# Spatial mixing woven into the projections of a one-core transformer kernel

## What is computed

```
h = rmsnorm(x, mix_norm)
q, k, v, su, sv, g_a, g_b = split(h @ w_in)
# chunked spatial gating: 4 chunks of 128 tokens, 8 groups of 64 channels
v = rmsnorm(gelu(sv), sgu_norm)
w = where(causal, w_s, 0)                                   # 8 x 128 x 128
mixed = einsum('gij,bcjgd->bcigd', w, v_chunks) + b_s
y_sgu = gelu(su) * mixed
y_att = sliding_window_attention(q, k, v, ...)              # 8 heads of 64, window 128
merged = sigmoid(g_a) * (y_att @ w_oa) + sigmoid(g_b) * (y_sgu @ w_ob)
x = x + merged @ w_out
```

## Time and profile before

| | |
|---|---|
| median of three runs | 1462.38 us |
| the profiled execution | 1462.21 us |
| its span, first to last instruction | 1460.5 us |
| busy: TensorE, VectorE, ScalarE, GpSimd | 1353.8, 779.4, 515.0, 605.4 us |
| mean granted TensorE clock | 0.978 |

### The profile page before, as it was taken

The page is one execution under the profiler, slowest core; times in us unless marked ns, Lnnn a source line. Parts: engine busy times, 40 slices in busy tenths (PEclk is TensorE's granted clock), DMA queues, the critical chain, the costliest instruction groups (busy, mean ns, idle before and its releaser), DMA issues.

```text
span 1460.5 us, 20168 instructions
## 1 busy us (share of the span) xinstructions
PE 1353.8 (93%) x6757; PEld 1085.5 (74%) x6757; DVE 779.4 (53%) x1526; ACT 515.0 (35%) x1084; POOL 605.4 (41%) x367
## 2 busy tenths in 40 slices
PE   4998799999899999999988699999979999999987
PEld 2765577687688888888867487777857888888866
DVE  3323667554455655641232467777524766666661
ACT  2222233411333333320111466666401544444420
POOL 3431133236344444465533244444244555555521
PEclk9999999999999999999999899999999999999999
DMA  5241122223133332333332011111123322222102
GB/s 150 79 95 44 44 72 58 72 59 101 58 101 98 89 100 87 100 105 94 94 98 72 14 45 44 29 43 43 29 77 92 97 69 70 68 68 68 57 20 82
DMA packets 196544, 105.38 MB, mean 72 GB/s; under 512 B 18974, under 2 KB 194428, under 8 KB 196492
## 3 DMA queue, kind: packets, MB, share of 16 engines
q1 hardware_dynamic: 195968, 103.98, 25.0%
q0 software_dynamic: 432, 0.69, 0.2%
q10 hardware_dynamic: 92, 0.02, 0.0%
HBM read 102.57 MB, written 2.10 MB: 72 GB/s over the span
## 4 chain that ended last, share of the span: by engine, by line
PE 78%; DVE 8%; issue 5%; ACT 4%; POOL 3%; DMA 1%; SPq 0%; DVEq 0%; POOLq 0%; ACTq 0%
PE ps L349 18%; PE ps L350 18%; PE ps L351 18%; PE ps L371 9%; PE ps L1164 1%; PE ps L1175 1%; POOL w_low L336 1%; PE ps L858 1%; DMA w_raw<-in_w_in_dram 1%; PE ps L1192 1%; PE ps L1194 1%; PE ps L1193 1%; POOL y_low L635 1%; PE ps L842 1%; DVE scaled L469 1%
## 5 line engine op out<-in xcount | busy, mean ns | idle before, releaser
L336 POOL TENSOR_TENSOR w_low<-w_raw,w_high 128x1024 fp32r<-128x1024 f32 x183 | 447.5, 2446 | 598.5 <-DVE w_high L331 598.4
L349 PE MATMUL ps<-h_high,w_high 128*128 128x512 f32 x864 | 353.4, 409 | 16.4 <-DVE h_low L473 11.6
L350 PE MATMUL ps<-h_low,w_high 128*128 128x512 f32 x864 | 344.0, 398 | 0.0
L351 PE MATMUL ps<-h_high,w_low 128*128 128x512 f32 x864 | 342.6, 397 | 0.0
L331 DVE CAST w_high<-w_raw 128x1024 fp32r<-128x1024 f32 x183 | 136.5, 747 | 154.8 <-PE ps L351 70.7
L349 PEld LDWEIGHTS ps<-h_high,w_high 128*128 128x128 f32 x864 | 164.1, 190 | 64.1 <-issue 20.3
L351 PEld LDWEIGHTS ps<-h_high,w_low 128*128 128x128 f32 x864 | 164.1, 190 | 37.6
L350 PEld LDWEIGHTS ps<-h_low,w_high 128*128 128x128 f32 x864 | 164.1, 190 | 35.3 <-issue 1.0
L1968 DVE SCALAR_TENSOR_TENSOR z<-ps,cv,z 128x511 f32<-128x511 f32 x44 | 33.0, 750 | 97.8 <-ACT z L1463 97.8
L1463 ACT ACTIVATE z<-ps,cv 128x512 f32<-128x512 f32 x44 | 34.3, 779 | 121.9 <-PE ps L351 121.7
L351 PE MATMUL ps<-m_high,w_low 128*128 128x512 f32 x176 | 69.4, 395 | 0.0
(11 more groups left out here) (326 smaller groups left out, 2541.8 us busy)
## 6 DMA issues: line engine op xcount, KB each, us to landing
w_raw<-in_w_in_dram SPq DMA_DIRECT2D x150, 256.0 KB, 3.2
w_raw<-in_w_up_dram SPq DMA_DIRECT2D x88, 256.0 KB, 3.2
w_raw<-in_w_out_dram SPq DMA_DIRECT2D x44, 256.0 KB, 3.0
w_raw<-in_w_down_dram SPq DMA_DIRECT2D x32, 256.0 KB, 3.1
w_raw<-in_w_down_dram SPq DMA_DIRECT2D x16, 192.0 KB, 2.6
rel<-in_rel_bias_dram SPq DMA_DIRECT2D x8, 384.0 KB, 3.1
x_tok<-in_x_dram SPq DMA_DIRECT2D x4, 512.0 KB, 5.6
w_raw<-in_w_oa_dram SPq DMA_DIRECT2D x8, 256.0 KB, 4.2
```

Source lines behind the costliest of these rows:

```text
L336: pool.tensor_tensor(w_low[:, n % RING, :], w_raw[:, n % RAW, :], w_high[:, n % RING, :].bitcast(F32), ALU.subtract).then_inc(low_made, 1)
L349: pe.matmul(acc, wh, mh, start=first and k == 0, stop=False)
L350: pe.matmul(acc, wh, ml, start=False, stop=False)
L351: done = pe.matmul(acc, wl, mh, start=False, stop=last and k == tiles - 1)
```

## The change

- The transposes of `ws_raw` go behind strip 5, into the middle of the su and sv strips; ACT copies them to `ws_t` between the squares of sv and the root of their sum.
- The sums no longer stand behind a projection but inside the next one: projection 1 is cut in four parts with one sv sum behind each; projections 2 to 5 are cut in two with the sum of the projection before between them. `qkv_sum` of the last one stands between the first two quarters of the mixing.
- sv is transposed in projections 4 and 5 (two chunks ahead of each, banks 2 and 3), and VectorE copies the chunks between its normalisations.
- Mixing (`mix`) does for each q and each chunk two matmuls of 64 output partitions and 128 columns, one for each group, so that a q fills one bank (2, 3, 7, 4) and four can be in flight. VectorE (`mixed`) adds the bias, multiplies, rounds and subtracts, each over all 128 partitions; ACT's rounding is gone. All `mix` calls are issued ahead of the first gate strip, with the first scores between the second and the third. VectorE prepares the attention bias ahead of `mixed(0)` and masks the first scores between `mixed(1)` and `mixed(2)`. TensorE's waits for the banks are spread over the first tiles.
- The merge uses w_ob before w_oa: its first strip waits only for the last masked scores, and the second for the whole attention output. The strips' order in memory loads and the banks follow.
- The small attention tensors no longer lie over `ws_raw` and `ws_t`.

```diff
@@ strip_sources
-                if m % 2 == 0:
+                if m % 2 == 1:
@@ tensor: su/sv strips
                 product(pe, ps[:, n % 4, :], n, 0, P, KT, hx).then_inc(strip_used, 1)
+                if n == 5:
+                    pe.wait_ge(s["ws_cut"], 1)
+                    pe.wait_ge(s["gain_ready"], 2)
+                    for g in range(8):
+                        mm = pe.transpose(ps[:, 6 + g // 4, (g % 4) * P:(g % 4 + 1) * P], ws_raw[:, g, :], ident[:])
+                    mm.then_inc(s["ws_turned"], 1)
@@ tensor: projections
+            def sv_turn(c):
+                if c == 0:
+                    pe.wait_ge(s["sv_normed"], 4)
+                elif c == 1:
+                    pe.wait_ge(s["v_ready"], 1)
+                else:
+                    pe.wait_ge(s["sv_tok_ready"], c - 1)
+                for k in range(4):
+                    mm = pe.transpose(ps[:, 2 + c % 2, k * P:(k + 1) * P], uv[:, 4 + k, c * P:(c + 1) * P], ident[:])
+                mm.then_inc(s["sv_turned"], 1)
+
+            cuts = [[(0, 8)], [(0, 3), (3, 5), (5, 7), (7, 8)], [(0, 5), (5, 8)], [(0, 4), (4, 8)], [(0, 4), (4, 8)],
+                    [(0, 4), (4, 8)]]
             for m in range(6):
                 n = N_QKV + m
                 pe.wait_ge(low_made, n + 1)
                 if m >= 4:
                     pe.wait_ge(s["i1_normed"], 1) if m == 4 else pe.wait_ge(s["v_copied"], 1)
-                product(pe, ps[:, bank[m], :], n, 0, P, KT, hx).then_inc(strip_used, 1)
-                if m == 0:
+                if m == 1:
                     pe.wait_ge(s["gelu_done"], 8)
-                    for k in range(4):
-                        sv_sum(k)
-                    qkv_sum(0)
                 elif m == 2:
...
+                    pe.wait_ge(s["ws_ready"], 1)
+                elif m == 4:
+                    sv_turn(0)
+                    sv_turn(1)
+                elif m == 5:
+                    sv_turn(2)
+                    sv_turn(3)
+                for part, ks in enumerate(cuts[m]):
+                    mm = product(pe, ps[:, bank[m], :], n, 0, P, KT, hx, ks=ks)
+                    if ks[1] == KT:
+                        mm.then_inc(strip_used, 1)
+                    if m == 1:
+                        sv_sum(part)
+                    elif m >= 2 and part == 0:
+                        qkv_sum(m - 2)
...
@@ tensor: mixing
+            MIX_BANK = (2, 3, 7, 4)
+
+            def mix(q):
+                if q < 2:
+                    pe.wait_ge(s["sv_tok_ready"], 4)
+                else:
+                    pe.wait_ge(s["i1_normed"], q + 1)
                 for c in range(4):
-                    mm = pe.matmul(ps[:, 2 + 2 * (q % 2) + c // 2, (c % 2) * 256:(c % 2) * 256 + 256],
-                                   uv_tok[:, c, q * P:(q + 1) * P],
-                                   ws_t[:, 2 * q:2 * q + 2, :].rearrange("p g i -> p (g i)"), start=True, stop=True)
+                    for h in range(2):
+                        mm = pe.matmul(ps[h * 64:(h + 1) * 64, MIX_BANK[q], c * P:(c + 1) * P],
+                                       uv_tok[:, c, q * P + h * 64:q * P + (h + 1) * 64], ws_t[:, 2 * q + h, :],
+                                       start=True, stop=True)
                 mm.then_inc(s["mixed"], 1)
...
+            mix(0)
+            qkv_sum(4)
+            mix(1)
+            pe.wait_ge(s["i1_root"], 5)
             a_scores(0, 0, first=True)
+            mix(2)
+            mix(3)
             with pe.Fori(0, 3) as j:
                 a_pair(j)
@@ tensor: merge
-            after(pe, "att")
+            pe.wait_ge(s["a_masked"], 32)
...
-                for b in range(2):
-                    n = N_MERGE + 2 * u + b
+                for turn, b in enumerate((1, 0)):
+                    n = N_MERGE + 2 * u + turn
                     pe.wait_ge(low_made, n + 1)
+                    if u == 0 and turn == 1:
+                        after(pe, "att")
@@ vector: mixing
+            def mixed(q):
                 dve.wait_ge(s["mixed"], q + 1)
...
+                part = scaled[:, q % 2, 0:S].rearrange("p (c i) -> p c i", c=4)
+                dve.tensor_tensor(part, ps[:, (2, 3, 7, 4)[q], :].rearrange("p (c i) -> p c i", c=4),
+                                  bias_s[:, q:q + 1, :].broadcast_to([P, 4, P]), ALU.add).then_inc(s["mix_biased"], 1)
+                dve.wait_ge(s["mix_biased"], q + 1)
+                dve.tensor_tensor(uv[:, q, :], uv[:, q, :], scaled[:, q % 2, 0:S], ALU.mult).then_inc(s["mix_gated"], 1)
+                dve.wait_ge(s["mix_gated"], q + 1)
+                dve.tensor_copy(a_high[:, 4 + q, :], uv[:, q, :]).then_inc(s["mix_high"], 1)
                 dve.wait_ge(s["mix_high"], q + 1)
                 dve.tensor_tensor(a_low[:, 4 + q, :], uv[:, q, :], a_high[:, 4 + q, :].bitcast(F32),
                                   ALU.subtract)
...
             a_bias(0)
+            mixed(0)
+            i1_norm(4)
+            mixed(1)
             a_masked(0, 0, N_GATE + 3)
+            mixed(2)
+            mixed(3)
```

More of the change, by code:

```diff
@@ L809, in _ @@
[L809 to L824, removed]
+                    pe.wait_ge(s["ws_ready"], 1)
[13 more added lines that the diff above has]
+                        qkv_sum(m - 2)
+                    if m == 2 and part == 0:
+                        pe.wait_ge(s["v_copied"], 1)
+                        for t in range(4):
+                            mm = pe.transpose(ps[:, 3, t * P:(t + 1) * P], v_f[:, t * P:(t + 1) * P], ident[:])
+                        mm.then_inc(s["v_turned"], 1)
@@ L865, in a_pair @@
                     pe.wait_ge(low_made, j * 4 + (N_GATE + t + 1))
+                    if t == 3:
+                        pe.wait_ge(s["i1_normed"], 5)
+                    elif t:
+                        pe.wait_ge(s["mix_biased"], t + 2)
                     product(pe, ps[:, GATE_BANK[t], :], N_GATE + t, 0, P, KT, hx, ks=(0, 7))
@@ L1360, in _ @@
                 act.activation(sq[:, k % 2, 0:S], uv[:, 4 + k, :], ACT.Square).then_inc(s["sv_sq"], 1)
+            act.wait_ge(s["ws_turned"], 1)
+            act.activation(ws_t[:].rearrange("p (b g) i -> p b (g i)", b=2), ps[:, 6:8, :], ACT.Copy)\
+                .then_inc(s["ws_ready"], 1)
             act.wait_ge(s["sv_sum"], 4)
@@ L1386, in _ @@
                 if j == 0:
-                    i1_root(0)
                     act.wait_ge(strip_used, N_QKV + 2)
                     act.activation(v_f[:], ps[:, 5, :], ACT.Copy).then_inc(s["v_copied"], 1)
-                elif j >= 2:
-                    i1_root(j - 1)
+                if j < 4:
+                    i1_root(j)
+            act.wait_ge(s["i1_normed"], 2)
+            act.activation(q_st[:], q_t[:, 0, :], ACT.Copy).then_inc(s["j_staged"], 1)
             i1_root(4)
-            after(act, "qkv")
-            act.wait_ge(s["ws_turned"], 1)
-            act.activation(ws_t[:].rearrange("p (b g) i -> p b (g i)", b=2), ps[:, 6:8, :], ACT.Copy)\
-                .then_inc(s["ws_ready"], 1)
-            for q in range(4):
-                if q == 2:
-                    act.wait_ge(s["mixed"], 4)
-                    act.activation(q_st[:], q_t[:, 0, :], ACT.Copy).then_inc(s["j_staged"], 1)
-                act.wait_ge(s["mix_gated"], 2 * (q + 1))
-                act.activation(a_high[:, 4 + q, :], uv[:, q, :], ACT.Copy).then_inc(s["mix_high"], 1)
             def a_pair(j, more=True):
```

45 lines of the change are left out of this document (13 added, 32 removed).

## The result

| | before | after |
|---|---|---|
| median | 1462.33 us of 4 runs | 1440.56 us of 4 runs (1438.17 to 1441.10) |
| the profiled execution, its span | 1462.21, 1460.5 us | 1438.17, 1436.4 us |
| mean granted TensorE clock | 0.978 | 0.979 |

The medians differ by 21.8 us. The ratio of the times over all runs, with its 95% interval, is 0.9841 [0.9829, 0.9854], which is 21.3 to 25.0 us of 1462.3. The prediction was 1441.7.

The account below looks back on a forecast made before the run. TensorE, 78% of the chain, was taken as the bound, with waits in the first fifth to remove. Gains of 14.5 + 6.1 = 20.6 us turned the 1460.5 span into 1439.9, 1441.6 of time, given as 1441.7; range 1435.5 to 1448.

Parts of the forecast that it names:

- Stage 1: Projections: sums lose their waits, but transposes moved in spend most of it; projection 5 ends at 129.4 against 130.3 us.
- Stage 2: Mixing to first attention tile: VectorE's queue comes last, first probabilities turned at 148.7 instead of 163.16 us, gain 14.5.
- The held product: In mixed(2), VectorE's product waits until GpSimd finishes strip 17's low part at 143.35: 1.2 us.
- Both collisions: GpSimd's low parts of strips 16 and 17 hold VectorE's second bias scaling and mixed(2)'s product; 3.0 us in all.
- The mixing: TensorE's matmuls for one mix(q), bounded by 1.0 and 4.0 us and taken as 2.0.
- Rival (b): TensorE bounds the mixing stage, with mix(q) of 4.0 us and 2 us of lower clock: 1447.5 us, chance 0.15.
- The clock: TensorE's pause from 144.8 to 148.7 drops its clock; the tail behind loses about 2.0 us, as before.
- rival (c): Clock stays at 1.2 GHz in the gate projections: 55 us slower if all 384 matmuls are slow, chance 0.03.
- The merge: First merge products start at 281.0 instead of 284.09: 3.1 us of wait and 3.0 of lower clock, gain 6.1.
- The sum: Total gain of the mixing stage and the merge: 14.5 + 6.1 = 20.6 us.
- (a): Collisions cost less or the clock survives a shorter pause: up to 3.0 + 2.0 us more gained, 1436.5, chance 0.2.
- Rival (d): Projections' transposes and copies hold VectorE, strips come late, only the merge's 6.1 us is left: 1456, chance 0.04.

Follow-up runs that it names:

- e9: The changed kernel with its sums put behind the projections again, as before the change: 1443.33 us, ratio 0.9864 to the kernel before.
- e3: The changed kernel with VectorE's scalings of the attention bias ahead of strip 16's rounding instead of behind it: 1441.51 us in one run.
- e5: The changed kernel with the rounding of the mixed values given back from VectorE to ScalarE: 1437.87 us in one run.
- e7b: The changed kernel with each mix's four matmuls of one half ahead of the other four, instead of alternating; second run of this kernel: 1439.19 us.
- e6: The changed kernel with 24 unread matmuls added in TensorE's pause ahead of the first turn of probabilities: 1440.88 us, ratio 0.9846 to before.
- e1: The kernel before with only the new order of the merge: 1460.81 us, ratio 0.9978 to the kernel before.
- e2: The changed kernel with the merge order of before: 1445.52 us, ratio 0.9880 to the kernel before.
- e4: The changed kernel with strip 16 rounded one normalisation earlier on VectorE: 1438.07 us, ratio 0.9821 to the kernel before.

## Why the prediction was right

**The bound** was read rightly: waits of the first fifth, more than TensorE's amount of work. Its busy time fell by 8.8 us (1353.8 to 1345.0), the span by 24.1.

**Stage 1.** Projection 1 was to end at 100.6, and its last sum ends there (99.73 + 0.86); the end of the fourth normalisation's last two copies was put at 130.4 and that of strip 16's rounding at 131.1, and they came at 129.54 and 130.13. Projection 5 ended at 128.96 (129.59 less the 0.63 idle), 0.4 ahead. The term mis-sized is the sum, 0.93 for 0.86 inside a stream of products. That the projections would end little earlier than before, though the sums' waits are gone, was right; e9 shows what the place of the sums is worth, 2.1 at the turn.

**Stage 2.** Predicted 148.7, measured 146.67: the gain is 16.5 instead of 14.5. The steps of the sum, in order: the queue is 1.0 ahead at strip 16's rounding; `mixed(0)` starts at 132.75, not at 134.3, another 0.5 because the held scaling ended with GpSimd's operation (130.21 + 2.40) and little behind it; a `mixed` takes 2.5, not 2.6, four times. The held product was put at 1.2 and took 1.1 more than its neighbours (1.82 against 0.69). Both collisions came where they were forecast, which GpSimd's row shows:

```profile
130.21 2.40 POOL L334 TENSOR_TENSOR w_low<-w_raw,w_high 128x1024 fp32r<-128x1024 f32 x1 [5.34 <-DVE w_high L329]
139.20 2.38 POOL L334 TENSOR_TENSOR w_low<-w_raw,w_high 128x1024 fp32r<-128x1024 f32 x1 [6.59 <-DVE w_high L329]
```

The operations that were held are those whose inputs all lie in SBUF, the scaling and the product; the bias adds from PSUM beside them kept their 0.69. The lock that the Trainium skill, "SBUF — State Buffer", describes in its section on the two separate sides agrees with the 2.71 and 1.82 here, and with the way in which e3 only moves the hold. The prediction cited the lock against the rounding taken from ScalarE; that was not what it hit: e5, with the rounding back on ScalarE, has the same 1.82.

**The mixing** was mis-sized by a factor of two: a mix(q) taken as 2.0 is 1.0, the lower bound of the prediction; for its upper bound of 4.0 it names no row, and the longest that a run shows is e7b's 1.5. It made no difference, for TensorE ended at 140.6 instead of 144.8 and waited 6.04 instead of 3.9 us; e6 and e7b show that neither 5.7 us of added matmuls nor mixes that are 0.5 longer reach the turn. Rival (b), TensorE as the bound, is out by a wide margin. Whether the drain at a change of tiling mode, of which the Trainium skill, "TensorEngine Tiling (Array Packing)", "Key Properties", speaks, takes part in this is open. The last sum stands between two groups of sixteen records (129.59, 130.61, 131.67) and takes 1.06 us up to the next group, against 0.86 for the sums inside a projection. The 0.2 can be a drain or weights that are loaded with nothing to hide behind, and no run tells them apart; it is small beside the 6.04 that TensorE waits.

**The clock** fell in the pause as supposed, its cost of 2.0 is seen in e6's profile, though not in its times, and rival (c), a clock that stays low through the gates, didn't occur: from 151.0 to 163.2 it is 1.00.

```profile
151.00:163.20 12.20, 12.20 (x57) 9.51 (x56) 8.13 (x22) 4.92 (x19) 4.58 (x2) 1.00 0.23 66
```

**The merge.** Predicted 6.1, measured 6.13 in B. That it came out to the tenth is partly luck: e1 and e2 put it at 5.2 and 4.8: in e2 the clock behind the old wait loses 1.4 us and not 3.0, in e1 another 0.8 are lost behind the turn. The prediction took the one length that the trace of before shows.

**The sum**, 20.6, met 21.8 between the medians of the result, 24.0 on the other chip, and 22.8 up to the end of the merge. It was about 2 too low, which is stage 2; that the medians came within 1.2 of it is in part the scatter of the runs. Some of the rivals' sums are slightly off in their own terms: (a) gives 1436.7, (b) 1447.8, (c) 56 us slower and with half of the matmuls 1480. Nothing rests on them. Rival (d), late strips in the projections, did not show: TensorE is busy 32.2 of the 33 us from 97 to 130.

How the 16.65 of A divide is shown in part only. The mixing starts 9.6 us earlier from the first point (85.7 before, 76.1 after), and the turn follows it 7.0 sooner (24.1, 17.1). Undone by themselves were the sums (2.1), the rounding on VectorE (0.8) and the order of the halves (nothing). Not undone by themselves were the early transposes of `ws_raw` and sv, and the mixed value in one full height instead of two. Of the 4.4 us that one took, ScalarE's part in the handover is 0.24 by e5; that the other 1.7 come from the operations saved is read from the two timelines, not tested.

## What to carry to other kernels

When one engine's queue ends a stage, list that queue in order with its durations and price everything else at nothing, up to the room that the other engines have: here 5.7 us of extra matmuls in a pause of 6.0 cost nothing at the turn, but once TensorE's mixing started 4.1 us later (e9), or VectorE's queue came 2.6 earlier (e4), VectorE waited for TensorE. Ask of each item in that queue whether the first consumer needs it: what brought most behind the change was to let the first tile pass ahead of half-finished work that nobody waits for. Place GpSimd's long operations where VectorE waits or reads PSUM, and take what a pause costs in clock as a range, since it differs between profiles of nearly the same program.

## What the runs showed of the hardware

- **Matmuls to two halves of the output rows are faster when they alternate.** Eight plain float32 matmuls of 128 columns with 64 output rows each take 1.0 us in the order low, high, low, high, and 1.5 us with the four of one half ahead of the other four (e7b, one profile). At the rate of the sums, 0.43 us for 512 columns of a record, they would take 1.7, an estimate.
- **The same 2.23 us of idle TensorE left the clock at 2.4 GHz in one profile and lowered it to 1.2 GHz in two others**, of a kernel whose instructions are the same up to there, and for 6 us (transposes of 1.97 instead of 1.09). Behind a wait of 3.1 us the lower level lasted 2.9 us in e2 and 6.4 in before.
- **A hold between GpSimd and VectorE falls on the next operation of VectorE whose inputs all lie in SBUF**: 2.71 for the two scalings instead of 0.61, or 2.26 on the product instead of 0.69 when the scalings are through (e3), or on nothing when VectorE is idle (strip 16's in e4). Bias adds with an operand in PSUM kept 0.69 beside it.
